# A hybrid decoder layer: low parts of the weight chunks written by VectorE, and an earlier split of the output weights in the last head

## The reference

```
h      = x * (1 + scale1) + shift1
q, k, v, u, gates = split(h @ w_in)
q, k   = rope(q), rope(k)
o      = (softmax(q1 k1) - lam * softmax(q2 k2)) @ v      per head, causal
a      = head_rmsnorm(o) * (1 - lam_init)
merged = sigmoid(g_pool) * pool_mixer(u) + sigmoid(g_attn) * a
x      = LN(alpha * x + (1 + gate1) * (merged @ w_out))
x      = LN(alpha * x + (1 + gate2) * HierMoE(x * (1 + scale2) + shift2))
```

## Time and profile before

| What | us |
| --- | --- |
| Median of 3 runs (1459.95 to 1461.92) | 1460.26 |
| The profiled execution | 1464.92 |
| Its span, first to last instruction | 1463.1 |
| PE busy | 1328.5 (91%) |
| DVE busy | 997.9 (68%) |
| ACT busy | 731.7 (50%) |
| POOL busy | 216.4 (15%) |

### The profile page before, as it was taken

One profiled execution on the slowest core, in us unless ns is written; L12 is line 12 of the kernel. 1 busy time (PEld: TensorE's weight loads), 2 busy tenths in 40 slices (PEclk: granted clock), 3 DMA queues, 4 the chain that ended last, 5 costly groups with the idle time before them and its releaser, 6 DMA issues.

```text
span 1463.1 us, 24663 instructions
## 1 busy us (share of the span) xinstructions
PE 1328.5 (91%) x8828; PEld 1134.6 (78%) x8828; DVE 997.9 (68%) x1503; ACT 731.7 (50%) x1285; POOL 216.4 (15%) x130
## 2 busy tenths in 40 slices
PE   6798979999999999999999976999469999999965
PEld 3488879989899889999989864778468887888721
DVE  1423527667676775757767665598659998999858
ACT  1334424445454544555435554332229898999712
POOL 1422211111111111111111000000011111111041
PEclk9889989999999999999999998999559999999987
DMA  8588233223322233323323433363167989556775
GB/s 304 181 282 265 88 95 112 79 81 111 93 84 82 83 102 93 103 70 96 90 84 107 121 112 105 104 215 123 65 215 273 354 293 370 188 200 207 267 221 157
DMA packets 210980, 229.43 MB, mean 157 GB/s; under 512 B 17942, under 2 KB 184794, under 8 KB 210747
## 3 DMA queue, kind: packets, MB, share of 16 engines
q1 hardware_dynamic: 195627, 173.39, 38.1%
q0 software_dynamic: 6976, 25.23, 5.5%
q10 hardware_dynamic: 8280, 29.51, 5.0%
HBM read 173.07 MB, written 46.79 MB: 150 GB/s over the span
## 4 chain that ended last, share of the span: by engine, by line
PE 76%; DVE 11%; ACT 4%; DMA 4%; issue 3%; SPq 2%; ACTq 0%; POOL 0%; DVEq 0%
PE AB L984 10%; PE AB L985 10%; PE AB L988 10%; PE S L911 6%; PE S L913 6%; PE S L912 6%; PE S L1080 4%; ACT F L1469 3%; PE T L1106 2%; PE OB L911 2%; PE OB L912 1%; PE OB L913 1%; PE S L926 1%; PE S L984 1%; PE OB L1330 1%
## 5 line engine op out<-in xcount | busy, mean ns | idle before, releaser
L1469 ACT ACTIVATE R<-F 128x1024 fp32r<-128x1024 f32 (+4 forms) x305 | 292.7, 1006 | 89.7 <-DVE F L2019 46.9
L984 PE MATMUL AB<-R 128*128 128x344 f32 x960 | 315.9, 333 | 0.0
L985 PE MATMUL AB<-R 128*128 128x344 f32 x960 | 304.8, 321 | 0.0
L911 PE MATMUL S<-R 128*128 128x512 f32 x480 | 192.1, 400 | 1.8 <-ACT F L1469 1.6
L913 PE MATMUL S<-R 128*128 128x512 f32 x480 | 188.3, 392 | 0.0
L912 PE MATMUL S<-R 128*128 128x512 f32 x480 | 187.8, 391 | 0.0
L984 PEld LDWEIGHTS AB<-R 128*128 128x128 f32 x960 | 182.0, 190 | 3.4 <-issue 3.2
L985 PEld LDWEIGHTS AB<-R 128*128 128x128 f32 x960 | 182.3, 190 | 1.7 <-issue 1.7
L2588 POOL TENSOR_TENSOR R<-F,R 128x1024 fp32r<-128x1024 f32 x40 | 99.2, 2480 | 568.0 <-ACT R L1469 568.0
L988 PE MATMUL AB<-R 128*128 128x344 f32 x960 | 171.6, 320 | 0.0
L988 PEld LDWEIGHTS AB<-R 128*128 128x128 f32 x960 | 155.7, 188 | 0.0
(11 more groups left out here) (281 smaller groups left out, 2383.1 us busy)
## 6 DMA issues: line engine op xcount, KB each, us to landing
F<-in_w_ada SPq DMA_DIRECT2D x24, 1024.0 KB
F<-in_w_in SPq DMA_DIRECT2D x44, 512.0 KB, 4.0
F<-in_w_e_gate SPq DMA_DIRECT2D x16, 1024.0 KB, 8.3
F<-in_w_e_up SPq DMA_DIRECT2D x16, 1024.0 KB, 11.7
F<-in_w_e_down SPq DMA_DIRECT2D x16, 1024.0 KB, 10.3
y_d<-F ACTq DMA_DIRECT2D x32, 512.0 KB, 7.7
out<-F SPq DMA_DIRECT2D x24, 512.0 KB, 4.1
F<-F SPq DMA_DIRECT2D x192, 43.0 KB, 1.9
```

What stands on the lines that cost most here:

```text
L911: mm(out, w[0], m[1], start=start, stop=False)
L984: mm(bank[:, 0:PIECE], whl[b][0][:, k, :], x[1][:, k, :], start=(k == 0), stop=False)
L985: mm(bank[:, 0:PIECE], whl[b][0][:, k, :], x[0][:, k, :], start=False, stop=False)
L1469: return nc.scalar.activation(out, in_, func, **kw)
```

## The change

In the heads, `chunk_lo` on VectorE takes over the low part of chunks 5 to 39 from GpSimd, which keeps chunks 0 to 4. VectorE does it behind the maxima of the step that follows the chunk's `split`. In the last head both pieces 4 and 5 are in step 4. The output weights k = 0 are split in step 4, 1 and 2 in step 5, 3 and 4 in step 6, 5 in step 7, 6 and 7 behind turns 6 and 7. TensorE does one unit and a half between each of the last four turns and products. SyncE issues `first_columns` ahead of the wait for `sT_done` and of the pages of values. No arithmetic is added or left out.

```diff
@@ step_pieces
         if h == H - 1:
-            return [first + i] if i < 6 else []
+            return [first + j for j in ((0,), (1,), (2,), (3,), (4, 5), (), (), ())[i]]
@@ SyncE, step 5
                         sp.dma_start(poolc, pool_d[h]).then_inc(poolc_landed, 16)
+                        if h == H - 1:
+                            first_columns()
                         sT_done.wait(sp, h, 0)
                         pages(h, cv, v_landed)
-                        if h == H - 1:
-                            first_columns()
@@ TensorE, behind the last step
         for n in range(6, 10):
             turn(H - 1, n)
-            unit(*((0, 4), (0, 5), (0, 6), (1, 0))[n - 6])
+            for of, k, halves in (((0, 4, (0, 1)), (0, 5, (0,))), ((0, 5, (1,)), (0, 6, (0, 1))),
+                                  ((1, 0, (0, 1)), (1, 1, (0,))), ((1, 1, (1,)), (1, 2, (0, 1))))[n - 6]:
+                unit(of, k, halves)
             product(H - 1, n)
-        for k in range(1, 4):
+        for k in range(3, 5):
             unit(1, k)
         squares(H - 1)
-        for k in range(4, 7):
+        for k in range(5, 7):
             unit(1, k)
@@ ScalarE (VectorE has w_out_lo and merged_lo in the same steps)
 step 4: page work, fillers, +w_out_hi(0)
 step 5: -w_out_hi(0), merged_hi(0), +w_out_hi(1), +w_out_hi(2)
 step 6: -w_out_hi(1) before weights(4), -w_out_hi(2), +w_out_hi(3), +w_out_hi(4), merged_hi(1)
 step 7: -w_out_hi(3), -w_out_hi(4), +w_out_hi(5) before sample_columns
         for n in range(6, 10):
             weights(H - 1, n)
-            if n < 9:
-                w_out_hi(n - 1)
+            if n < 8:
+                w_out_hi(n)
@@ VectorE, heads
+        def chunk_lo(h, i):
+
+            for g in step_pieces(h, i):
+                c = g // 3 + 2
+                if g % 3 == 2 and c < N_CHUNKS:
+                    if c == 5:
+                        dve.wait_ge(w_lo.sem, U_CHUNKS + 5)
+                    dve.wait_ge(w_landed[c % 2], raw_landed(c))
+                    dve.wait_ge(w_hi.sem, U_CHUNKS + c + 1)
+                    TT(whl[c % 2][1], wraw2[c % 2], whl[c % 2][0].bitcast(F32), ALU.subtract).then_inc(w_lo.sem, 1)
@@ VectorE, each step
                 maxima(h, i)
+                if i:
+                    chunk_lo(h, i - 1)
+                elif h:
+                    chunk_lo(h - 1, 7)
@@ GpSimd
-        for c in range(1, N_CHUNKS):
+        for c in range(1, 5):
             chunk_rest(c)
```

More of the change, by code:

```diff
@@ L1756, in _ @@
                     filler()
+                    if h == H - 1:
+                        w_out_hi(0)
                 if i == 5:
@@ L1762, in _ @@
                     if h == H - 1:
-                        w_out_hi(0)
                         merged_hi(0)
+                        w_out_hi(1)
+                        w_out_hi(2)
                 if i == 6:
@@ L1768, in _ @@
                     filler()
-                    if h == H - 1:
-                        w_out_hi(1)
                     weights(h, 4)
@@ L1773, in _ @@
                     if h == H - 1:
-                        w_out_hi(2)
+                        w_out_hi(3)
+                        w_out_hi(4)
                         merged_hi(1)
@@ L1781, in _ @@
                     filler()
-                    if h == H - 1:
-                        w_out_hi(3)
                     outputs(h, 2)
@@ L1787, in _ @@
                     if h == H - 1:
-                        w_out_hi(4)
+                        w_out_hi(5)
                     sample_columns(h)
@@ L2274, in _ @@
                     page_scores(h)
+                    if h == H - 1:
+                        w_out_lo(0)
                 if i == 5:
@@ L2280, in _ @@
                     if h == H - 1:
-                        w_out_lo(0)
                         merged_lo(0)
+                        w_out_lo(1)
+                        w_out_lo(2)
                 if i == 6:
@@ L2286, in _ @@
                     combine(h, i)
-                    if h == H - 1:
-                        w_out_lo(1)
                     pool_gate(h, 1)
                     if h == H - 1:
-                        w_out_lo(2)
+                        w_out_lo(3)
+                        w_out_lo(4)
                         merged_lo(1)
@@ L2297, in _ @@
                     combine(h, i)
-                    if h == H - 1:
-                        w_out_lo(3)
                     pool_gate(h, 2)
                     if h == H - 1:
-                        w_out_lo(4)
+                        w_out_lo(5)
         for n in range(6, 10):
             weights(H - 1, n)
-            if n < 9:
-                w_out_lo(n - 1)
+            if n < 8:
+                w_out_lo(n)
         merged_lo(2)
```

## The result

The changed kernel took 1453.1 us (median of 5 runs, 1451.07 to 1455.8) against 1461.63 of the kernel before beside it (5 runs, 1459.95 to 1464.7): ratio 0.9941, 95% interval 0.9928 to 0.9954. The forecast was 1452.8 with a range of 1449.8 to 1457.2. In a later session it took 1452.98 (7 runs) against 1462.14, ratio 0.994 [0.9918, 0.9961]. So the number was right; of the steps that led to it, several were not.

A forecast was written before the change was run, and what follows sets the result against it. TensorE's stream was taken to bound seven heads, leaving the last head's second half to win. Terms 0 - 6.3 (the +0.5 within it) - 1.2 + 0 = -7.5 us, from the median 1460.3 to 1452.8, range 1449.8 to 1457.2.

The forecast's parts named there:

- Part 1: Heads: moving 35 low parts of chunks from GpSimd to VectorE changes the time by 0 us, range -1 to +2.
- the 29 us of rows 7: Heads, line 2135 on VectorE: 64 instances take 39.4 us, 10.2 without GpSimd's subtractions, so VectorE gets 29 us back.
- the floor of -1: Heads: at most about 1 us gained, since a head leaves 0.88 us in 90 to win on TensorE.
- Rival (c): Heads gain as well: short waits for low parts go, 7 x 0.5 = 3.5 us, 1449.3; chance 0.07.
- Part 2: Last head, steps 4 and 5: maxima(5) begin about as before, maxima(6) 0.5 to 0.7 us later; +0.5 us.
- Part 3: Last head, steps 6 and 7: maxima(7) 2.3 us sooner, turn 6 at 895.5; -6.3 us in all to turn 6.
- rival (b): Around turns 5 and 6: half rate and late tile 3 columns cost up to 3.9 us, 1456.7 at most; chance 0.17.
- behind turn 5 that hides behind VectorE: Last head: units slowed at half the clock, 1.37 to up to 2.7 us, cost nothing more on the path.
- Part 4: The last four turns: with 1.5 units between, waits for splits go, less 0.2 for extra starts; -1.2 us.
- Part 5: Behind the turns: tile 3's columns hold with 0.2 us of slack and the rest moves as a block; 0 us.
- rival (d): After the turns: merge, its store and column loads set the end, so the gain is given back, 1458.7; chance 0.07.
- Rival (a): Heads: VectorE's added work shows, two exposed positions cost 16.8 us, 1469.6; chance 0.04.

The follow-up runs named there:

- gap_splits: The changed kernel with VectorE's output-weight splits moved into its idle gaps in the last head: 1446.34 us (6 runs), 1445.32 in the next session.
- last_only: The changed kernel with only the last head's part; low parts of the chunks stay on GpSimd: 1451.46 us, ratio 0.9926 to the kernel before.
- whole_units: The changed kernel with one whole unit between each of the last four turns and products, as before: 1451.91 us, ratio 0.9936 to the kernel before.
- double_low: The changed kernel with each of VectorE's 35 low parts in the heads written twice: 1477.69 us, ratio 1.0108.
- late_columns: The changed kernel with the columns of tiles 0 and 1 loaded behind the pages of values, as before: 1453.74 us, ratio 0.9943.
- old_splits: The kernel before with only both last pieces in step 4 and the early columns: 1460.2 us, ratio 0.9986.
- gap_gpsimd: gap_splits with the 35 low parts of the chunks back on GpSimd: 1446.71 us, against 1445.32 for gap_splits beside it.
- heads_only: The kernel before with only the heads' part, VectorE writing the low parts of chunks 5 to 39: 1458.49 us against 1461.95, ratio 0.9978.
- one_split: The kernel before with one line moved, w_out_lo(1) between weights 3 and 4 of the last head's step 6: 1458.74 us, ratio 0.9968.

## Why the prediction was right, and where it was not

**Part 1, the heads: 0.** Measured -1.49 for the seven, of which 1.2 is head 3 and the others are 0.02 to 0.11 each (the 0.11 is head 0, within its spread): outside the -1 by half a us. The cover held at all five positions, also in step 7, where I had left 0.1 us. That the 29 us of rows 7 are VectorE's time alone was right. The step that failed is the floor of -1: it came from one stretch, in head 5, taken for every head, and from line 2135 as the only operation that GpSimd stretches. Operations of `combine` are stretched too, and in head 3 one was on TensorE's path. The marks of all heads would have shown that one head is 1.2 longer than the others. Rival (c) named a gain but not this one: it had seven times 0.5 for short waits, and those stayed: from 200 to 815 us TensorE waits 3.8 us for line 2151, 6 times, against 4.5, 7 times, before, and the one that is gone is the 0.67 of head 3. A small misreading besides: of the waits of 1.69, 5.86 and 3.19 us the first is for the merged rows (line 2224) and is none of the 9.2 us for line 2219; no term rests on it.

**Part 2, steps 4 and 5: +0.5 with `maxima(5)` where it was.** From `maxima(5)` to `maxima(6)` it was 9.13 us against 8.68, so two splits and `merged_lo(0)`, where there were one split and `merged_lo(0)`, cost 0.45, as worked out. But `maxima(5)` came 1.35 later. The step that failed is that the second piece is through at 862.6 - 818.2 = 44.4 and `w_out_lo(0)` at about 47. The first half of the piece ran at half the clock: behind the wait of 1.79 us in step 4 (at 852.92) the granted clock was 0.50 from 854 to 856 us, and over stretches of 5 us

```profile
850.00:855.00 5.00, 3.21 (x20) 2.96 (x19) 3.71 (x7) 3.19 (x8) 0.00 (x0) 0.88 0.40 119
855.00:860.00 5.00, 5.00 (x28) 5.00 (x28) 4.29 (x7) 0.59 (x2) 0.00 (x0) 0.78 0.87 261
```

The kernel before has the same wait of 1.79 us (at 857.35), and there the stretch is at the full clock (it fell behind the next wait, the 2.38 us at 861.12, and was 0.50 from 862 to 866, ahead of a step with one piece):

```profile
855.00:860.00 5.00, 1.95 (x14) 1.46 (x12) 3.67 (x8) 3.48 (x8) 0.00 (x0) 1.00 0.47 153
```

So the split ended at 862.3, 48.5 behind h7, and `maxima(5)` stood behind it. The scores of step 5, which TensorE issues behind that piece, were through only some 0.4 us sooner. The repeat of gap_splits shows both: the clock fell in it as well, and its `maxima(5)`, with no split ahead of it, waited 2.46 us for TensorE and started at 48.10, against 0.89 us and 46.50 in the execution in which the clock did not fall:

```profile
861.51 1.76 DVE L2131 TENSOR_REDUCE sm<-S 128x2 f32<-128x1536 f32 x1 [2.46 <-PE S L1083]
```

```profile
859.11 1.76 DVE L2131 TENSOR_REDUCE sm<-S 128x2 f32<-128x1536 f32 x1 [0.89 <-PE S L1083]
```

So the clock is nearly all of the 1.35, and the split in front of `maxima(5)` at most 0.4. I had priced the clock for later gaps only.

**Part 3, turn 6: -6.3.** Measured -4.47. From `maxima(6)` to `maxima(7)` it was 13.22 us, worked out 13.1; from there to the end of `combine(7)` 7.11, worked out 7.1. These terms were right. What went wrong is 1.35 at `maxima(5)`, above, and 0.56 behind `combine(7)`, where I left 0.6 and the trace has 1.16: TensorE still had its own queue between the page columns (turn 5, at 884.76) and turn 6 to do, at a clock of 0.63 and 0.52. Product 5 started at 888.11, though its low part was there at 887.49: 0.6 us, as much as is missing.

```profile
884.00:886.00 2.00, 1.24 (x5) 0.97 (x6) 1.93 (x5) 0.09 (x1) 0.00 (x0) 0.63 0.00 0
886.00:888.00 2.00, 2.00 (x6) 0.72 (x5) 1.49 (x2) 1.58 (x3) 0.00 (x0) 0.52 0.00 0
```

last_only shows that the two don't add. Its piece ran at the full clock, `maxima(7)` came 2.5 us sooner than before, about the forecast's 2.3, and yet turn 6 was only 0.3 ahead of the change's, 2.3 us behind `combine(7)`: from turn 5, which follows the page columns (881.74), to turn 6 (891.04) TensorE took 9.3 us there, 8.1 in the change and 7.65 in gap_splits, and its clock in last_only was

```profile
882.00:884.00 2.00, 2.00 (x8) 1.03 (x8) 2.00 (x2) 0.68 (x2) 0.00 (x0) 0.50 0.00 0
884.00:886.00 2.00, 2.00 (x8) 1.31 (x7) 0.48 (x1) 2.00 (x3) 0.00 (x0) 0.50 0.04 8
```

This is rival (b)'s mechanism, at some 2 us of its 3.9: 0.6 behind turn 5, where I had put it, and the rest in step 4, where I had not. The assumption that failed is "behind turn 5 that hides behind VectorE". The Trainium skill, TensorE: Matmul & The Clock Gate, section "Why this matters for your kernels", warns of idle gaps between bursts. The rows bear it out behind the waits of 3.40 us in the change (0.63 and 0.52) and 3.70 in last_only (0.50); behind the shorter one of 1.79 us the clock fell in some executions and not in others.

**Part 4, the turns: -1.2.** Measured -1.24, by the change against whole_units. The starts of the four turns agree with the mechanism. They are 2.92, 2.83 and 2.85 us apart before and 2.93, 2.83 and 2.84 in whole_units, so the order of the splits makes no difference there; in the change half a unit more, 0.69 us of work, stands between, and they are only 0.3 to 0.4 further apart (3.23, 3.25, 3.21), with no gap left on TensorE.

**Part 5, what follows: 0.** It held. ScalarE still waited for TensorE ahead of tile 3, 7.39 us where it was 8.79, and for no DMA; rival (d) is out. In all kernels the rest moved as a block within its spread.

**The sum.** -7.5 forecast; by the marks -7.2, from 1.5 that I had not forecast and 5.7 where I had 7.5: turn 6 came 4.5 us sooner and not 6 to 7, tile 3 5.7 and not 7 to 8. The number is as near as it is because two misses cancel, which is luck. Rival (a) never showed; double_low shows what it would have taken: not one length of 1.2 us at a place, but a second. Of the signs named, the others held: line 2137 at 0.16 us throughout, 5 subtractions left on GpSimd, no wait of TensorE for low parts of the output weights.

**A step that I did not see.** The forecast took the order of the change as given: two splits and `merged_lo(1)` ahead of `page_columns`, where TensorE waits for them. I even had that term (3.8 us, and 0.8 for the columns) and wrote it down as "the same four as before". gap_splits shows that this work fits in the gap of 3.18 us and others, and that 4.3 us between the two maxima were there to win. A second one stands on ScalarE ahead of turn 6, in the trace of the change:

```profile
891.48 1.06 ACT L1471 ACTIVATE R<-F 128x1024 fp32r<-128x1024 f32 x1
892.57 0.18 ACT L1471 ACTIVATE F<-T 128x8 f32<-128x8 f32 x1
```

The first is `w_out_hi(5)`, the second the sample's columns, for which turn 6 then waits 0.99 us. What moving the first behind the second would give, no run shows; at most 1.06 us.

## What to carry to other kernels

Work that an engine does for later belongs in the gaps in which that engine waits for another, ahead of what the others need next from it: the same splits on the same engine, only in its gaps, gave 6.6 us more than the change. When one engine's wait is blamed on an order elsewhere, move that one line first: here it gave 3.5 us, against 5.7 for everything in the last head. And compare all repeats of a stage by a common mark, not one of them: a single head that is 1.2 us longer than its sisters is invisible in sums and in medians.

## What the runs showed of the hardware

**The order of two starts decides who waits, for a whole instruction.** GpSimd's subtraction 0.08 us ahead makes VectorE's operation 3.01 us and not 0.88, in five kernels and always in head 3; in head 5 it starts 0.16 behind, and the subtraction takes 3.00 and not 2.41. The Trainium skill, SBUF — State Buffer, section "Who interferes with whom", says as much of such pairs; what I had not expected is how exactly it repeats, and that of some 33 us of stretched operations one, of 2.1, cost 1.2 us and the rest nothing that shows.

**The clock falls behind a wait in one execution and not in another of the same kernel.** gap_splits and its repeat have the same wait of 1.79 us in step 4. Granted clock in the stretch behind it, in the first execution and in the second:

```profile
852.00:856.00 4.00, 4.00 (x30) 4.00 (x29) 3.10 (x7) 1.61 (x4) 0.00 (x0) 1.00 0.58 148
```

```profile
852.00:856.00 4.00, 3.45 (x17) 3.48 (x18) 2.67 (x7) 2.45 (x6) 0.00 (x0) 0.69 0.57 181
```

`maxima(5)` comes at 46.50 in the one and 48.10 in the other, and tile 3 at 101.96 and 103.59, so this is worth 1.6 us there. In the traces of the change, twice, and of late_columns, whole_units and double_low it fell, in those of last_only, old_splits and gap_gpsimd it did not. It may be no mere chance. Counting `before`, heads_only and one_split, which have the same wait of 1.79 us and one piece behind it, the clock fell there in 7 of the 8 executions in which VectorE writes the low parts in the heads, and in none of the 5 in which GpSimd does. Then the 1.35 us at `maxima(5)` would be a price of the heads' part, and last_only's median, no higher than the change's, would fit. With one trace or two of each kernel, and gap_splits once with and once without the fall, this isn't shown; what decides it stays open.
